# A transformer kernel's first norm: gain applied behind the transposes, and the first weight tiles loaded ahead

## The reference, cut to what matters

```python
def rms_norm(x, g):
    xf = x.astype(jnp.float32)
    y = xf * lax.rsqrt(jnp.mean(xf * xf, axis=-1, keepdims=True) + EPS)
    return (y * g.astype(jnp.float32)).astype(x.dtype)

def swiglu(h, w_gate_up, w_down):
    a, b = jnp.split(h @ w_gate_up, 2, axis=-1)
    return (jax.nn.silu(a) * b) @ w_down

x = x + 0.5 * swiglu(rms_norm(x, ffn1_norm), ffn1_w_gate_up, ffn1_w_down)
```

## Time and profile before

| | |
|---|---|
| Median of 3 runs | 1447.02 us |
| Profiled execution | 1446.91 us, its span 1445.1 us |
| TensorE matmul busy | 1436.6 us (99%) |
| VectorE busy | 986.7 us (68%) |
| ScalarE busy | 820.6 us (57%) |
| HBM read | 265.36 MB, 184 GB/s over the span |

### The profile page before, as it was taken

How to read it: one execution, slowest core, us unless ns; L and a number is a source line. 1 busy time by engine, 2 the same in 40 slices (tenths; PEclk the granted TensorE clock), 3 DMA queues, 4 the chain that set the end, 5 groups by cost and what they waited for, 6 DMA issues and landing times.

```text
span 1445.1 us, 20910 instructions
## 1 busy us (share of the span) xinstructions
PE 1436.6 (99%) x8064; PEld 1231.0 (85%) x8064; DVE 986.7 (68%) x1604; ACT 820.6 (57%) x1414; POOL 143.7 (10%) x212
## 2 busy tenths in 40 slices
PE   9999999999999999999999999999999999999999
PEld 7888888898888888888888898888888899888887
DVE  6666667776666666666676677666677867778775
ACT  6555556754655555555466746555557665455553
POOL 0100024000000001000050003000038200100000
PEclk9999999999999999999999999999999999999999
DMA  8756555354655646565564455555546335446551
GB/s 331 250 191 195 182 200 193 122 194 168 217 189 190 192 140 237 192 199 178 174 233 140 162 180 205 189 190 193 185 164 224 127 117 182 159 172 222 198 185 49
DMA packets 73682, 267.77 MB, mean 185 GB/s; under 512 B 8176, under 2 KB 8304, under 8 KB 73456
## 3 DMA queue, kind: packets, MB, share of 16 engines
q1 hardware_dynamic: 73296, 265.65, 54.7%
q10 hardware_dynamic: 288, 0.79, 0.1%
HBM read 265.36 MB, written 1.05 MB: 184 GB/s over the span
## 4 chain that ended last, share of the span: by engine, by line
PE 97%; ACT 1%; DMA 1%; DVE 0%; issue 0%; SPq 0%; ACTq 0%
PE bank L553 30%; PE bank L558 15%; PE bank L506 9%; PE bank L507 9%; PE bank L508 8%; PE bank L567 4%; PE bank L572 4%; PE bank L568 4%; PE bank L536 3%; PE bank L543 3%; PE bank L537 3%; PE bank L526 1%; PE bank L698 1%; PE bank L722 1%; PE bank L709 1%; DMA raw<-w_dram 1%
## 5 line engine op out<-in xcount | busy, mean ns | idle before, releaser
L1567 DVE TENSOR_TENSOR wlo<-raw,whi 128x1024 fp32r<-128x1024 f32 (+1 forms) x481 | 580.2, 1229 | 15.1 <-ACT whi L1038 15.0
L1038 ACT ACTIVATE whi<-raw 128x1024 fp32r<-128x1024 f32 (+1 forms) x481 | 497.5, 1050 | 3.5 <-PE bank L572 1.8
L553 PE MATMUL bank<-hx,whi 128*128 128x512 f32 x1856 | 468.5, 393 | 0.0
L553 PEld LDWEIGHTS bank<-hx,whi 128*128 128x128 f32 x1856 | 338.4, 188 | 66.5 <-issue 3.0
L558 PEld LDWEIGHTS bank<-hx,wlo 128*128 128x128 f32 x1856 | 253.1, 190 | 18.3
L558 PE MATMUL bank<-hx,wlo 128*128 128x256 f32 x1856 | 258.7, 282 | 0.0
L506 PE MATMUL bank<-whi,hid 128*128 128x512 f32 x536 | 211.2, 394 | 0.2 <-issue 0.2
L507 PE MATMUL bank<-wlo,hid 128*128 128x512 f32 x536 | 209.9, 392 | 0.0
L508 PE MATMUL bank<-whi,hid 128*128 128x512 f32 x536 | 208.6, 389 | 0.0
L1067 ACT ACTIVATE hid<-prod 128x256 fp32r<-128x256 f32 x126 | 52.7, 418 | 167.3 <-DVE prod L1671 108.9
L508 PEld LDWEIGHTS bank<-whi,hid 128*128 128x128 f32 x536 | 100.7, 188 | 21.8
(11 more groups left out here) (241 smaller groups left out, 1518.7 us busy)
## 6 DMA issues: line engine op xcount, KB each, us to landing
raw<-w_dram SPq DMA_DIRECT2D x486, 512.0 KB, 4.0
gain<-g_dram SPq DMA_DIRECT2D x7, 512.0 KB, 3.8
arena<-c_dram SPq DMA_DIRECT2D x2, 768.0 KB, 6.4
cst<-c_dram SPq DMA_DIRECT2D x1, 1056.0 KB, 7.0
out_dram<-x SPq DMA_DIRECT2D x4, 256.0 KB, 2.0
par<-p_dram SPq DMA_DIRECT2D x1, 867.0 KB, 8.6
raw<-w_dram SPq DMA_DIRECT2D x2, 432.0 KB, 3.5
gain<-g_dram ACTq DMA_DIRECT2D x1, 512.0 KB, 4.7
```

The lines of the kernel that those rows point to most:

```text
L553: e.matmul(b[:, :], hi_of(j)[:, k * P:k * P + P], hx[:, k * 2 * S:k * 2 * S + 2 * S], start=k == 0, stop=False, skip_group_check=True)
L1038: e.activation(hi_of(t), raw_of(t), ACT.Copy).then_inc(sem["w_hi"], 1)
L1567: e.tensor_tensor(lo_of(t), raw_of(t), hi_of(t).bitcast(F32), ALU.subtract).then_inc(sem["w_lo"], 1)
```

## The change

Stage 0 alone is changed (n == 0), and the loads at the begin.

- The norm weights come as eight columns, `gcol`, 128x8 fp32, packed into a free corner of an array that is there already. ScalarE's queue loads them in the place of `gain`. The later stages load `gain` as before; its semaphore counts one load less.
- `norm_x` multiplies x by rstd alone, with a `tensor_scalar`.
- `norm_hi` and `norm_lo` multiply by the column of the feature block. As each feature block has its own column, a bank's eviction is four instructions of 128 columns instead of one of 512, on ScalarE and again on VectorE. The semaphore is raised by the last of the four.
- SyncE issues tile 1 ahead of x of block 1.
- On ScalarE and VectorE the work on tile 0 stands ahead of the evictions of block 0, and the two evictions follow each other.

```diff
@@ sp_program
-                if j == 0:
+                if j == 1:
                     e.dma_start(x[:, D:2 * D], x_in[P:2 * P, :]).then_inc(sem["ld_x1"], 16)
@@ norm_hi
                     b = bank[K.BANK["xt", n, a, g][0]]
+                    if n == 0:
+                        E.wait_ge("ld_g0", 16)
+                        for k in range(4):
+                            ins = e.activation(feat(0, g, a)[:, k], b[:, k * P:k * P + P], ACT.Copy, scale=gcol[:, 4 * g + k:4 * g + k + 1])
+                        ins.then_inc(sem["xhi"], 1)
+                        continue
                     e.activation(feat(0, g, a), by4(b[:, :]), ACT.Copy).then_inc(sem["xhi"], 1)
@@ act_program
             e.dma_start(xq(0, 1), x_in[0:P, 512:1024]).then_inc(sem["ld_x01"], 16)
-            e.dma_start(gain[:, :], gains[0]).then_inc(sem["ld_gain"], 16)
+            e.dma_start(gcol, gains[8][:, 512:512 + KD]).then_inc(sem["ld_g0"], 16)
             squares(0, 0, 0)
-            norm_hi(0, 0, (0,))
             hi_upto(0)
-            norm_hi(0, 0, (1,))
+            norm_hi(0, 0)
             hi_upto(1)
@@ norm_x
-                E.wait_ge("ld_gain", 16 * n + 16)
+                E.wait_ge("ld_gain", 16 * n)
                 for h in range(2):
+                    if n == 0:
+                        e.tensor_scalar(xnq(a, h), xq(a, h), st[:, 4 * a + 2:4 * a + 3], None, ALU.mult).then_inc(sem["xn"], 1)
+                        continue
@@ norm_lo
+                    if n == 0:
+                        E.wait_ge("ld_g0", 16)
+                        for k in range(4):
+                            ins = e.scalar_tensor_tensor(feat(1, g, a)[:, k], b[:, k * P:k * P + P], gcol[:, 4 * g + k:4 * g + k + 1],
+                                                         feat(0, g, a)[:, k].bitcast(F32), ALU.mult, ALU.subtract)
+                        ins.then_inc(sem["xlo"], 1)
+                        continue
@@ dve_program
             norm_x(0, 0)
-            norm_lo(0, 0, (0,))
             lo_upto(0)
-            norm_lo(0, 0, (1,))
+            norm_lo(0, 0)
             lo_upto(1)
@@ pack_gains
     for l in range(2):
+        out[8, :, 512:512 + KD] = g("ffn1_norm")[0].reshape(KD, P).T
```

More of the change, by code:

```diff
@@ L334, in build_program @@
         st = small[:, 0:12]
+        gcol = small[:, 192:200]
         sqj = arena[:, 0:2048]
@@ L385, in build_program @@
         col8 = lambda ap: ap.rearrange("p (h o) -> p h o", o=1)
-        DMAS = ([f"raw{i}" for i in range(NRAW)] + ["ld_x00", "ld_x01", "ld_x1", "ld_gain", "ld_i", "ld_c", "ld_p", "ld_pw", "ld_pm"]
+        DMAS = ([f"raw{i}" for i in range(NRAW)] + ["ld_x00", "ld_x01", "ld_x1", "ld_gain", "ld_g0", "ld_i", "ld_c", "ld_p", "ld_pw", "ld_pm"]
                 + [f"st{a}{h}" for a in range(2) for h in range(2)])
```

## The result

| | median, us | runs | range |
|---|---|---|---|
| before | 1446.67 | 20 | 1446.40 to 1447.36 |
| changed | 1448.83 | 20 | 1447.42 to 1450.49 |

The ratio is 1.0014, its 95% interval 1.0008 to 1.0020. The changed kernel is 2.16 us slower, less than the 2.9 us that I had called distinguishable, but clear of its interval, and outside the range of 1446.1 to 1448.2. The spread is news as well: 3.1 us from run to run, where before has 1.0. It goes with TensorE's granted clock, averaged over the whole run. Five runs with a mean clock of 1.000 took 1447.42 to 1448.09 us, ten with 0.999 took 1448.57 to 1449.28, two with 0.998 took 1448.69 and 1449.10, three with 0.997 took 1450.28 to 1450.49.

The account below looks back on a forecast made before the run. The start of block 1's first matmul was taken to bound the kernel, TensorE being busy after it. Reaching it at 17.88 instead of 17.93 made 1446.91 into 1446.9; with 0.11 for the median, 1447.0 us, range 1446.1 to 1448.2.

Parts of the forecast that it names:

- Where the end is decided: Block 1's first matmul decides the time; forecast at 17.88 against 17.93 before, with TensorE's later work in unchanged order.
- The wait in front of it that was forecast: TensorE, after tile 3 of block 0, waits 0.6 to 1.0 us for block 1's low parts.
- The loads: At the begin, 512 KB less in front lands tile 0 near 6.3 instead of 7.5, 1.25 us sooner.
- rival B: Tile 0 lands late, so its rounding on ScalarE delays block 0's evictions: block 1 at 18.8, 1447.9 us; chance 0.13.
- rival C: TensorE's clock drops after a 2.2 us gap before block 0's first matmul: 1447.9 us, held longer near 1449.5; chance 0.07.
- The pieces: Stage 0 evictions of four 128-column pieces: 1.18 us instead of 0.60 on ScalarE, 1.13 instead of 0.64 on VectorE.
- Rival A: Stage 0 evictions' cost does not show; TensorE goes from tile 3 into block 1 at 17.1: 1446.2 us; chance 0.18.
- the way from transpose to matmul: From block 1's transposes to its first matmul: 3.09 us, through ScalarE's evictions and VectorE's low parts.
- Later stages: After block 1's first matmul, one stream of TensorE work in unchanged order; new waits there would make the forecast wrong.
- The bound of what can be told: A measurement of this kernel tells a change from none at about 0.2%, 2.9 us; same was given 0.96.

Follow-up runs that it names:

- both cures: Changed kernel with columns in the identity's rows, tile 0 on ScalarE's queue, and ten more matmuls on zeros behind block 0's transposes: 1447.02 us.
- the run that held the clock: Changed kernel with 14 more matmuls on zeros on TensorE behind block 0's transposes: 1447.71 us.
- the hybrid: The both cures kernel with gain as a row for block 1, loaded on SyncE's queue behind tile 3, and block 1's evictions whole: 1446.58 us.

## Why the prediction was wrong

- **Where the end is decided:** right. The loss is the shift of block 1's first matmul, 2.08 us of the 2.16. The wait in front of it that was forecast (0.6 to 1.0 us) is there, 0.60.
- **The loads:** wrong, and the step that failed. The prediction took each 512 KB in front of tile 0 as worth 1.25 us and put the landing at 6.3; it was 7.73. What the two queues moved in the first microseconds was not one sum: ScalarE's queue carried gain at a rate that SyncE's alone did not take over. The steps of 1.25 us that I had read were true of neighbours on SyncE's queue at the 417 GB/s of the stretch from 6.30 on the earlier trace rows, and I applied them to another queue's bytes in the microseconds before, where the changed kernel moved 0.77 MB in 3 us, 255 GB/s. Nor did tile 0's landing go by the bytes in front of it even on its own queue. The small evictions then began at 8.71 instead of 7.63, and wlo of tile 2 ended at 15.25 instead of 14.28: 0.97 us. With tile 0 at 6.1 (tile 0 on the second queue, and both cures) this was gone. It is rival B, which I had priced at 0.9 us and given 0.13. I had both bounds of the landing in the sum and then worked with the one end; the nearest measured landing, 7.5, was the other.
- **The clock:** rival C came with it. The gap was 3.40 us and not 2.2, as the late tile lengthened it, and the slow matmuls kept block 1's transposes from 15.7 to 17.01: 1.25 us in the profile, 1.1 in the medians. I treated B and C as alternatives; B made C likelier, and the two add: 17.88 + 0.97 + 1.25 - 0.09 (the way from transpose to matmul took 3.00, not 3.09) = 20.01. The 1.25 is what is left when the 0.97 is taken off, so the sum can't miss; what checks it is the run that held the clock, with block 1 1.29 us sooner. The prediction also read both clock levels out of the first warm-up matmuls (421 and 275 ns); in the kernel before the granted clock is 1.00 from 1 to 6 us, so the rows don't show that this difference is the clock's. The Trainium skill, TensorE: Matmul & The Clock Gate, Part 1: The HAM clock gate, says that an idle stretch brings the half clock back; the trace agrees (3.40 us still, then 0.51, and in two experiments the fall within the still time). It also fell after a gap of 1.95 us.
- **The pieces:** right in size. Eight evictions held ScalarE from 8.71 to 10.71, 2.00 us (2.16), four low parts took 1.13 to 1.14 (1.13); the norm product 0.44 a half (0.47). In the kernel before they cost 1.64 us, an unknown part of it by the clock; the kernel with both cures, with its sooner loads, shorter norm product and held clock, is 0.38 above before. Rival A did not come: even without B and C there is no gain, as what is won at the transposes goes into the way behind them. One sum was slightly off: the way is 1.18 + 1.13 - 0.60 - 0.64 = 1.07 us longer than before, not 1.03.
- **Later stages:** right. TensorE waited for the same things in them as before, 0.7, 0.5 and 0.3 us.
- **The bound of what can be told:** 2.9 us was too coarse. With 20 runs each 2.16 us stood clear.

## What to carry to other kernels

Bytes taken off one DMA queue at the begin of a program need not be time given to another: count by queue what each moves, and try the first tile needed on the queue that has become free. A short wait that lengthens TensorE's still time has a second price, the clock; rivals that feed each other are to be added, not listed side by side. And a factor by partition behind a transpose turns one eviction into as many as there are blocks, which costs most where the engine behind has nothing else to do.

## What the runs showed of the hardware

- A load of 128 rows of 32 bytes (4 KB) in front of a 512 KB load on the same queue delayed that by 3 to 3.5 us at the program's begin (gain used at 9.41 instead of 6.30; tile 0 at 9.63 instead of 6.10). Between 3.5 and 6.5 us the other queue moved 0.38 MB instead of 0.64 in the second case, but 0.58 instead of 0.63 in the first. As the last thing on its queue it made no difference to be seen (tile 0 at 7.73 with it, 7.83 with the columns in the identity's rows). Why isn't settled.
- SyncE's queue alone moved 0.70 to 0.75 MB between 3.5 and 6.5 us, and 1.18 to 1.26 MB in the 3 us after that. What holds it at the begin wasn't tried. Tile 0 landed at 7.53 and 7.73 though the queue had moved 1.12 and 1.22 MB by 7 us, and what stands up to tile 0's end is 0.85 MB.
- The mean granted clock was below 1.000 in 15 of 20 runs of the kernel whose profile has a gap of 3.40 us, in 4 of 11 and 5 of 11 with gaps of 1.95 and 1.96 us, in 7 of 11 with 1.79 us, and in none of the 93 runs of the kernel before that ran beside the experiments (1.12 us). The gaps are those of one profiled run each, and with 1.96 us that run kept its clock. So the length of the gap alone does not order the kernels. Between the matmuls on zeros at the begin and the gap TensorE ran only the eight transposes of block 0, 1.05 to 1.23 us; what these do for the clock wasn't tried.
- In the changed kernel's profile the clock fell 1.3 us or more after work had begun again, and for about 3.4 us. Where TensorE had stood still for longer (gain as well as columns; the small load in front of tile 0) it fell within the still time, at about 8.6 and 12.3 us.
- Matmuls on zeros in the gap kept the mean at 1.000 in all of 33 runs, those of the hybrid among them.
